# Shifting four groups of high-half and low-half copies between iterations of an attention loop

## The reference

```python
q, k, v, bg, cg, u = _project(xs * (1 + ca) + sa, w_in[l])
att = _latent_attention(q, k, v, cache_k[:, l], cache_v[:, l], rpb[l])   # 8 heads
mix = _merge(att, _short_conv(bg, cg, u, conv_w[l]), w_out[l])           # concat(att, conv) @ w_out
xs = _layer_norm(ALPHA * xs + ga * mix, ln1_g[l], ln1_b[l])
```

## Time and profile before

| | |
|---|---|
| time, median of 3 runs | 623.72 us (622.5 to 625.28) |
| the profiled execution | 625.28 us |
| its span, first to last instruction | 623.2 us |
| busy: TensorE, VectorE, ScalarE, GpSimd | 87%, 59%, 43%, 15% |
| mean granted TensorE clock | 0.955 of full |
| attention loop, first row maximum to first output-projection product | 250.33 to 320.34 us |

### The profile page before, as it was taken

How to read it: one execution, slowest core, us unless ns; L and a number is a source line. 1 busy time by engine, 2 the same in 40 slices (tenths; PEclk the granted TensorE clock), 3 DMA queues, 4 the chain that set the end, 5 groups by cost and what they waited for, 6 DMA issues and landing times.

```text
span 623.2 us, 8075 instructions
## 1 busy us (share of the span) xinstructions
PE 540.9 (87%) x3226; PEld 445.4 (71%) x3226; DVE 367.7 (59%) x577; ACT 267.2 (43%) x368; POOL 91.9 (15%) x121
## 2 busy tenths in 40 slices
PE   3798999999989989778979999959999999996371
PEld 0476888998669989556768888938888888784120
DVE  1236131444002030798838987879999998985295
ACT  1326130202103121787730213167888888762141
POOL 0005600002100000233000000031221222200611
PEclk9977999999989999999989999889999999997797
DMA  8996994475915212299149200688999999983756
GB/s 288 396 314 173 262 357 160 141 265 162 337 59 182 106 48 90 52 366 263 33 143 355 77 35 34 238 332 311 392 395 419 420 422 398 387 290 131 262 154 123
DMA packets 54974, 146.01 MB, mean 234 GB/s; under 512 B 7288, under 2 KB 16051, under 8 KB 48792
## 3 DMA queue, kind: packets, MB, share of 16 engines
q1 hardware_dynamic: 41368, 109.46, 48.3%
q0 software_dynamic: 10832, 34.43, 17.1%
q10 hardware_dynamic: 2736, 1.61, 0.9%
HBM read 127.07 MB, written 23.35 MB: 241 GB/s over the span
## 4 chain that ended last, share of the span: by engine, by line
PE 61%; DMA 13%; DVE 10%; issue 9%; ACT 5%; SPq 1%; POOL 0%; ACTq 0%; POOLq 0%; DVEq 0%
PE PS L1523 9%; PE PS L1525 8%; PE PS L1524 8%; PE PS L1578 7%; PE PS L1579 7%; PE PS L1583 7%; DMA uni<-in_w_expert_out 5%; PE PS L1540 3%; DMA raw<-in_w_ada 2%; DMA g<-in_x_prompt 2%; PE PS L1774 2%; PE PS L1831 2%; PE PS L1761 1%; DMA uni<-h_rows,uni 1%; PE PS L1675 1%
## 5 line engine op out<-in xcount | busy, mean ns | idle before, releaser
L1523 PE MATMUL PS<-w_hi,act_hi 128*128 128x512 f32 x248 | 101.2, 408 | 4.9 <-DVE act_lo L1296 2.5
L1578 PE MATMUL PS<-act_hi,w_hi 128*128 128x320 f32 x320 | 100.2, 321 | 2.6 <-ACT g L714 1.7
L1579 PE MATMUL PS<-act_lo,w_hi 128*128 128x320 f32 x320 | 98.3, 315 | 0.0
L1525 PE MATMUL PS<-w_hi,act_lo 128*128 128x512 f32 x248 | 97.7, 394 | 0.0
L1524 PE MATMUL PS<-w_lo,act_hi 128*128 128x512 f32 x248 | 97.4, 393 | 0.0
L1583 PE MATMUL PS<-act_hi,w_lo 128*128 128x320 f32 x320 | 74.3, 314 | 0.0
L1286 DVE TENSOR_TENSOR w_lo<-raw,w_hi 128x2048 fp32r<-128x2048 f32 x32 | 73.0, 2287 | 1.4 <-ACT w_hi L860 0.6
L1578 PEld LDWEIGHTS PS<-act_hi,w_hi 128*128 128x128 f32 x320 | 62.0, 194 | 9.1 <-issue 4.5
L860 ACT ACTIVATE w_hi<-raw 128x2048 fp32r<-128x2048 f32 x32 | 61.1, 1913 | 10.3 <-DMA raw<-in_w_expert_in 6.3
L1579 PEld LDWEIGHTS PS<-act_lo,w_hi 128*128 128x128 f32 x320 | 62.0, 194 | 0.0
L1523 PEld LDWEIGHTS PS<-w_hi,act_hi 128*128 128x128 f32 x248 | 47.3, 191 | 17.0 <-issue 5.6
(11 more groups left out here) (232 smaller groups left out, 871.5 us busy)
## 6 DMA issues: line engine op xcount, KB each, us to landing
raw<-in_w_expert_in SPq DMA_DIRECT2D x32, 1024.0 KB, 12.6
raw<-in_w_ada SPq DMA_DIRECT2D x24, 1024.0 KB, 8.5
uni<-in_w_expert_out SPq DMA_DIRECT2D x16, 1024.0 KB, 12.6
raw<-in_w_in SPq DMA_DIRECT2D x12, 1024.0 KB, 8.3
expert_rows<-uni POOLq DMA_DIRECT2D x16, 512.0 KB, 8.0
expert_rows<-g POOLq DMA_DIRECT2D x2, 2560.0 KB, 11.8
g<-in_x_sample SPq DMA_DIRECT2D x2, 2048.0 KB, 15.0
raw<-in_w_out SPq DMA_DIRECT2D x4, 1024.0 KB, 7.5
```

The costliest lines, as they stand in the source:

```text
L1523: T.matmul(out, lh, rh, start=first, stop=False)
L1525: return T.matmul(out, ll, rh, start=False, stop=last)
L1578: T.matmul(out, a, h_hi[:, k, sl], start=f, stop=False)
L1579: T.matmul(out, a, h_lo[:, k, sl], start=False, stop=False)
```

## The change

Two conditions in ScalarE's loop and one in VectorE's are changed. In ScalarE's loop the two halves of the last weight chunk's `split_hi` go from iterations 1 and 2 to iterations 2 and 3, and the four `conv_hi` parts from iterations 3 to 6 to iterations 4 to 7. `mix_hi` is left where it was, in iterations 6, 10 and 14. In VectorE's loop `mix_lo` for groups 0, 1 and 2 goes from iterations 7, 11 and 15 to iterations 6, 10 and 14; `split_lo` and `conv_lo` stay in iterations 2, 3 and 4 to 7.

```diff
@@ -808,10 +808,10 @@
                 if 1 <= v <= NV:
                     copy_pt(v - 1)
 
-                if v in (1, 2):
-                    split_hi(NW - 1, (v - 1,))
-                if v in (3, 4, 5, 6):
-                    conv_hi(v - 3)
+                if v in (2, 3):
+                    split_hi(NW - 1, (v - 2,))
+                if v in (4, 5, 6, 7):
+                    conv_hi(v - 4)
                 if v >= 6 and (v - 6) % NB == 0 and v - 6 < PAIRS:
                     mix_hi((v - 6) // NB)
             mix_hi(HP)
@@ -1143,8 +1143,8 @@
                     split_lo(NW - 1, (v - 2,))
                 if v in (4, 5, 6, 7):
                     conv_lo(v - 4)
-                if v >= 7 and (v - 7) % NB == 0 and v - 7 < PAIRS - NB:
-                    mix_lo((v - 7) // NB)
+                if v >= 6 and (v - 6) % NB == 0 and v - 6 < PAIRS:
+                    mix_lo((v - 6) // NB)
             mix_lo(HP - 1)
             mix_lo(HP)
```

## The result

| | before | after |
|---|---|---|
| median | 624.0 us | 633.78 us |
| ratio after / before | | 1.0145 (95% interval 1.0114 to 1.0175) |
| profiled execution, its span | 625.28, 623.2 us | 629.12, 627.0 us |
| row maximum of iteration 0 starts | 250.33 us | 246.49 us |
| row maximum of iteration 8, after that of 0 | 32.56 us | 39.93 us |

The account below looks back on a forecast made before the run. The attention loop was taken as the bound, paced by VectorE up to iteration 8 and TensorE later. Terms 0.97 + 2.15 + 4.36 + 1.67 = 9.15 us on 623.72 gave 632.9 us, range 630.0 to 636.5.

Parts of the forecast that it names:

- the sum: Loop terms: iteration 2 +0.97, iteration 3 +2.15, iterations 4 to 7 +4.36, groups 1 and 2 +1.67; 9.15 us together.
- What bounds the kernel: Attention loop: VectorE sets the pace up to iteration 8; it reaches extra work at 2.86 us, ScalarE at 3.08.
- the prediction's own sign of being wrong: Iteration 8 starting before 288 us would refute the premise that both engines reach the extra work together.
- The low halves of groups 1 and 2: Moving them to iterations 10 and 14 costs 0.90 and 0.77 us; rival that they cost nothing: 631.2 us, chance 0.11.
- `mix_lo(0)` was free, as costed: Group 0's low half, moved from iteration 7 to 6, costs nothing in itself, with a cover of 0.04 us.
- The clock: TensorE's gaps of about 4 us in iterations 2 and 3 make its clock fall; 0 us in the forecast.
- The rival of a clock that stays low: TensorE's clock stays low through iteration 9 and costs 1 to 3 us: 635.0 us, chance 0.17.
- The tail: After the loop nothing starts at a fixed time, so the 9.15 us are passed on in full.
- Bias loads: GpSimd's loads in the loop: 0 us taken; rival that they come 1 to 2 us late: 634.5 us, chance 0.06.
- Not slower: VectorE's wait runs in TensorE's shadow in iterations 2 to 7, leaving only gains: 621.7 us, chance 0.04.
- its point of decision: Whether TensorE's work per iteration exceeds VectorE's 4.76 us; the rows before gave 3.19 us.

Follow-up runs that it names:

- the apart runs: Two runs of the kernel before, each with one edit: mix_lo of group 2 in iteration 14, or of group 1 in iteration 10; 624.9 and 627.13 us.
- low-halves-only run: The kernel before with only VectorE's half of the change, mix_lo of groups 0 to 2 in iterations 6, 10, 14; ratio 1.0028.
- late fill: The kernel before with the 5 MB fill of the overflow rows issued after iteration 11's bias load instead of iteration 3's; ratio 1.0009.
- mended spread version: The kernel before with split_hi's first half before the loop, mix_lo in 9, 12, 16 and the overflow fill after iteration 11's bias load; ratio 0.997.
- group 2 run: The kernel before with one edit, mix_lo of group 2 in iteration 14 instead of 15; 624.9 us, executed once.

## Why the prediction was right

By its steps, all lengths from one row maximum to the next:

| iteration | before | predicted | measured |
|---|---|---|---|
| 2 | 6.25 | 7.22 | 7.25 |
| 3 | 5.07 | 7.22 | 7.19 |
| 4 | 3.67 | 4.76 | 4.77 |
| 5 | 3.67 | 4.76 | 4.71 |
| 6 | 3.66 | 5.56 | 5.56 |
| 7 | 4.50 | 4.76 | 4.71 |
| 10 | 3.11 | 4.69 | 4.72 |
| 11 | 3.67 | 2.86 | 2.86 |

Iterations 2 to 7 together gained 7.37 us against the 7.48 of the sum. Iterations 8 to 15 gained 68.26 − 39.93 − (59.23 − 32.56) = 1.66 against 1.67. To iteration 16 that is 9.03 against 9.15, and the ratio puts the whole at 9.05 us.

**What bounds the kernel:** right. The premise that ScalarE begins a high half 0.2 us after VectorE is ready for the low half shows in each wait, which is about the copy's length plus 0.1 to 0.2 (2.09 and 2.03 for 1.92, 1.01 for 0.85). By its letter the prediction's own sign of being wrong came true, as iteration 8's row maximum started at 286.42 us, before 288. But that sign was written as a time of the whole span, and the changed execution was 3.84 us ahead before the loop. Counted from iteration 0, the limit was 288 − 250.33 = 37.67 us, and 39.93 was measured.

**The low halves of groups 1 and 2:** the sum was right, and the apart runs give 0.65 and 1.06 for what was taken as 0.77 and 0.90. That the transposes carry some of the delay on holds for group 1. `mix_lo(0)` was free, as costed, but only because the convolution copy held VectorE longer: alone, in the low-halves-only run, it cost 0.94 us.

**The clock:** the fall was foreseen, and that it would be covered in iterations 3 to 5. The gap was 3.82 us where 4 were expected; the second was 2.49, since TensorE's own work was slowed and filled it. No row maximum waited for scores there, but the cover was thin: in iteration 3 TensorE worked 274.66 − 269.93 = 4.73 us, up to the transposes of iteration 4, without a pause, and iteration 4 lasted 4.77. The rival of a clock that stays low and costs 1 to 3 us did not come.

**The tail:** this step failed. I took the time from iteration 16's row maximum to the first output-projection product as unchanged. It was 324.13 − 314.75 = 9.38 instead of 10.78 us, 1.40 shorter, as the clock did not fall in iteration 16. So 77.64 − 70.01 = 7.63 us stand in the two profiles at a place where 9.15 were forecast. It is not a gain of the change that can be counted on: the tail came out at 9.37 and at 10.78 us with the same lists and gaps of 2.99 and 2.98 us. The ratio over all executions is nearer the forecast than this pair of profiles. That the forecast of the whole lies within 0.1 us of it is partly luck, since the clock moves loop and tail by 0.7 and 1.4 us from one execution to the next, and the executions that weren't profiled are unknown. What decides the level stays open.

**Bias loads:** right that they cost nothing. The 0.36 us wait of before is gone, as its user comes later; it waits 0.61 us for scores instead.

**Not slower:** its point of decision, TensorE's work above 4.76 us an iteration, was not reached, if only by 0.03 us.

## What to carry to other kernels

When one engine's output is another's input in a software-pipelined loop, check in which iteration each stands: a copy an iteration ahead is hidden, unless it holds up its own engine's next work (the first weight copy did, by 1.18 us), and the same copy in the same iteration is paid in full, as the two engines take turns. Work out when each engine reaches its extra work, counted from one common row, before moving either. After a loop is made faster, look for the loads and buffer releases that its old pace hid, and judge a change of a few microseconds by distances within its stage, since executions here differ by several microseconds ahead of it.

## What the runs showed of the hardware

TensorE's clock fell after idle gaps shorter than I had expected from the kernel before. A gap of 1.94 us ahead of iteration 4's transposes left them at 1.09 us in the kernel before, and at 1.09 to 1.10 us in three other runs. The same gap at the same place was followed by 1.72 and 1.67 us in the two runs that moved one group, by 1.79 us with the late fill and by 1.89 us in the mended spread version, though in three of these four the lists of TensorE, VectorE and ScalarE are, up to there, those of the kernel before:

```profile
270.45 1.72 PE L1675 MATMUL PS<-const,uni 128*128 128x128 f32 x8 [1.94 <-ACT uni L787]
```

This row is from the group 2 run. Each such fall cost 0 us where the iteration was long, about 0.7 us at iteration 6, and 1.49 us at iteration 9 of the low-halves-only run, with 0.52 of it given back. So a loop with idle gaps of 2 us carries a cost that comes and goes with the execution.

The other is the price of GpSimd beside VectorE: a 128x512 normalisation of 0.49 us took 3.99, 3.16 and 5.21 us while GpSimd subtracted, and the maxima that read PSUM were not slowed.
